# State outputs of both steps of a tile together, the chain's value in PSUM, and the output projection begun beside the last attention block

## The chip, the cores and the metric

One program runs on one core of a Trainium2 chip. The metric is the device time of one execution in microseconds, as the median of several runs. Five engines work side by side and wait for each other on semaphores: TensorE (PE; its weight loads are listed apart as PEld), VectorE (DVE), ScalarE (ACT), GpSimd (POOL), and SyncE (SP), which issues most transfers.

## The reference

The kernel computes a chain of transformer-like blocks over a sequence of 512 positions and a width of 1024: an attention block with compressed and windowed keys ("nsa"), a state-space block ("s5"), and a second network (a stick-breaking and retention mixer, a convolutional feed-forward, a gated linear attention mixer, and again a feed-forward). The change touches the end of the first block and the second. In short form:

```python
h = x + nsa_mixer(rmsnorm(h, l0_norm), ...)        # ends with  mix @ l0_w_out
# s5 mixer, with u, z = split(rmsnorm(h, l1_norm) @ l1_w_in)
#   per 32 channels: complex diagonal state, 
#   state[t] = lambda_bar * state[t-1] + B_bar u[t]
#   y[t] = Re(C state[t]) + D u[t]
#   out = glu(gelu(y) @ l1_w_glu) * silu(z) @ l1_w_out
h = h + s5_mixer(rmsnorm(h, l1_norm), ...)
```

## The kernel before

**Weights.** All weight matrices are cut into tiles of 128 output features by 1024 inputs. SP streams them into a ring of four buffers `raw` (`sp_stream`, `sp_tiles`). For each tile DVE makes the rounded high part (`split_tile`, `whi`, L171), POOL subtracts it from the original to get the low part (`wlo`, L151, L163, L1688, L2496), and TensorE makes 24 multiplications per tile: eight chunks of the inputs by three (high by high, high by low, low by high). `whi` and `wlo` have two buffers each, so the cast of tile t+2 waits until tile t is done (`tile_done`). The accumulators are PSUM banks 0 and 1.

**The attention block.** Eight pairs of heads by four blocks of queries make 32 steps M (`pe_macro`, `act_macro`, `dve_macro`). In each step TensorE turns the probabilities (L1277), and multiplies them by the values (L1289), with quarters of a projection tile put between (`pe_beside`); steps 30 and 31 have no such tile. After the last step ACT takes the gate (`act_nsa_z`, L1428, with two activation tables loaded), DVE multiplies (`dve_mix`, `nmix`), ACT makes the high half (`act_nsa_hi`, `nh`), and POOL the low half (`rest`, `nl`, L1702). POOL's low parts of the first two tiles of the output projection come after that, in its general stream.

**The output projection** ("nsa_out", `pe_residual`, `dve_residual`): eight tiles m, each of 24 multiplications. After each tile DVE casts the tile after next, adds to the residual `h` (L401), adds a square (L237), and does a piece of the preparation for the state-space block, `s5_setup(dve, j)` after tile j. A piece is a complex product of "taps": two multiplies of 128x1024 elements into `wtmp` (`tap_product`, L2168) and two sums of 128x512. Pieces 0 to 3 are the input taps, piece 4 the first output taps; before piece 0 come eight small copies (`tap_coefficient`). The raw taps are fetched by two transfers on ACT's queue (`act_s5_loads`), issued when tile 0 is done. Then the norm begins (L288).

**The state-space block.** Eight input tiles (`input_tile`) give `su`; SP shuffles each with 16 small transfers into `ub`. DVE goes on with taps and tables between the casts. The loop has 16 steps g, two for each tile f = g // 2 of 128 channels. In each step TensorE computes the inputs to the states of the next step (`pe_inputs`, L2533), DVE runs the chain (`s5_chain`, L2401 to L2419): multiply by a rotation `se`, a scan along time (L2408), multiply back, and write the states `sx`. TensorE then adds the outputs of the states (`pe_states`, L2556) into bank 6. That is, per step, 16 multiplications of 128 moving columns, each split into two instructions, for two groups q of 32 output rows in turn. On the side TensorE turns the next tile's taps (`pe_taps_turn`, L2506, even steps), makes its short kernels (`pe_kernels`, L2517 and L2519, odd steps), multiplies them in (`pe_lags`, L2543, odd steps), and does half of a further projection tile (`product_beside`, L595 to L597, 12 multiplications per step). ACT empties the banks, POOL makes the rotations (`pool_s5`, six operations of 128x256 per step) and one `wlo` per tile. After the loop come the gated unit (L2598) and the output.

In each step of the chain DVE waits for the step before; `sx` has one buffer for each parity of g.

Of the kernel before, what the change touches and what calls it, by code (L numbers as in the profile page):

```python
# [9 lines left out]
ALU = mybir.AluOpType  # L10
# [37 lines left out]
def build(nc, A, out, names=tuple(s[0] for s in STAGES)):  # L48
# [5 lines left out]
    with ExitStack() as ctx:  # L54
# [27 lines left out]
        epsc = tables[:, 2 * P:2 * P + 1]  # L82
        base = (nc.sbuf_base + 63) // 64 * 64
# [1138 lines left out]
        def pe_beside(pe, M, half):  # L1222

            if nsa_tile(M) is None:
                return
# [11 lines left out]
            if second == 1 and half == 1:  # L1237
                mm.then_inc(tile_done, 1)

# [108 lines left out]
        def act_nsa(act):  # L1348
# [62 lines left out]
            act_nsa_z(act, PAIRS - 1)  # L1411
# [53 lines left out]
        def act_macro(act, M):  # L1465
# [6 lines left out]
            if m == 2 and i < PAIRS - 1:  # L1472
                act_nsa_q(act, i + 1)
            if m == 3 and i < PAIRS - 1:
                act_cmp_exp(act, i + 1)
# [206 lines left out]
        def pool_nsa(pool):  # L1682
# [24 lines left out]
            for i in range(PAIRS):  # L1707
# [5 lines left out]
                if i < PAIRS - 1:  # L1713
                    low(7 + 2 * i)
            rest(PAIRS - 1)
# [439 lines left out]
        def act_s5_loads(act):  # L2155
            act.wait_ge(tile_done, T0["nsa_out"] + 1)
# [113 lines left out]
        def tap_product(dve, to, frm, re, im, conj):  # L2270

            (to_re, to_im), _ = taps_of(to, conj)
            _, x = taps_of(frm, conj)
            for k, coef in enumerate((re, im)):
                a = twice[:, coef].rearrange("p f c q -> p f (c q)").rearrange("p f (e h) -> p f e h", h=1)
                tt(dve, tap_tmp[k], x, a.broadcast_to([P, KC, 8, 16]), ALU.mult)
            by_re, by_im = tap_tmp
            tt(dve, to_re, by_re[:, :, 0:4, :], by_im[:, :, 4:8, :], ALU.add if conj else ALU.subtract)
            tt(dve, to_im, by_re[:, :, 4:8, :], by_im[:, :, 0:4, :], ALU.subtract if conj else ALU.add)

# [22 lines left out]
        def s5_input_taps(dve, j):  # L2303

            if j == 0:
                for k, v in enumerate((cre, cim, abre, abim)):
                    tap_coefficient(dve, k, v)
                dve.wait_ge(s_bc, 32)
                tap_product(dve, 0, 0, t_cre, t_cim, False)
            else:  # L2310
                tap_product(dve, j, j - 1, t_are, t_aim, False)
# [62 lines left out]
        def s5_setup(dve, j):  # L2374

            if j < 4:
                s5_input_taps(dve, j)
            if j == 4:
                s5_output_taps(dve, 0)
                s5_output_taps(dve, 1)  # L2380
# [3 lines left out]
        TURN, KERN = (4, 5), 7  # L2384
# [6 lines left out]
        def s5_chain(dve, g):  # L2391

            a, b = sp_[:], sb_[:]
            e_r, e_i = (se[:, g % 2, c:c + 1, :].broadcast_to([P, 2, 2 * KB]) for c in range(2))
# [6 lines left out]
            nc.vector.tensor_tensor(a, bu, e_r, ALU.mult)  # L2401
# [621 lines left out]
```

## Time and profile before

| | |
|---|---|
| median of 3 runs | 2085.98 us (2081.94 to 2087.9) |
| profiled execution | 2086.61 us, span of its records 2084.8 us |
| TensorE busy | 1981.5 us, 95% of the span |
| DVE / ACT / POOL busy | 55% / 29% / 39% |
| end of the attention to the norm | 365.9 to 432.0 us |
| state-space loop | 500.9 to 635.2 us |

Times in the rows are us from the start of the span. An engine's busy time counts a weight load apart. The number in brackets is how long the engine sat idle before the instruction, and what ended it. Ends of TensorE's multiplications are modelled, so their starts are what is compared.

### The profile page before, as it was taken

What the parts mean: (1) busy time and instruction counts of PE and PEld (TensorE: products, weight loads), DVE (VectorE), ACT (ScalarE), POOL (GpSimd) and SP (SyncE); (2) the same over time, 40 slices, a digit from 0 to 9 for tenths busy, and PEclk for the clock granted to TensorE, in tenths of its full rate; (3) what the DMA queues carried; (4) which work ended last, traced back from release to release, by engine and by line L of the source; (5) the groups of instructions that cost most, each with busy time, mean ns of one, the idle gap of its engine ahead of it and who ended that gap; (6) DMA issues with size and microseconds to landing.
All of it is one profiled execution on the core that took longest, in us unless ns stands there. A gap on an engine that the chain in (4) does not pass through costs nothing.

```text
span 2084.8 us, 26851 instructions
## 1 busy us (share of the span) xinstructions
PE 1981.5 (95%) x9924; PEld 1549.0 (74%) x9924; DVE 1143.3 (55%) x2063; ACT 608.3 (29%) x1164; POOL 813.7 (39%) x430
## 2 busy tenths in 40 slices
PE   8999999778999997999999999999999999999999
PEld 5867776656777875666768888888578878888887
DVE  5679998676994434555455454512443355454411
ACT  3136655134552114445422111100322222111100
POOL 3532221345773442222224444444233334444444
PEclk9999999998999998999999999999999999999999
DMA  5620100212102222111112232233212222232232
GB/s 185 172 68 32 41 32 21 91 57 62 65 31 71 91 93 84 51 51 61 61 61 93 91 101 93 99 104 109 67 67 81 71 80 93 91 101 92 99 131 71
DMA packets 55300, 167.64 MB, mean 80 GB/s; under 512 B 8080, under 2 KB 16144, under 8 KB 54816
## 3 DMA queue, kind: packets, MB, share of 16 engines
q1 hardware_dynamic: 47904, 155.22, 22.5%
q10 hardware_dynamic: 7296, 11.08, 1.9%
q8 instruction: 65, 1.06, 0.2%
q14 instruction: 35, 0.29, 0.0%
HBM read 157.88 MB, written 2.10 MB: 77 GB/s over the span
## 4 chain that ended last, share of the span: by engine, by line
issue 40%; PE 33%; POOL 15%; DVE 11%; ACT 1%; POOLq 0%; DVEq 0%; ACTq 0%
POOL wlo L163 14%; PE bank L180 7%; PE bank L181 7%; PE bank L182 7%; DVE prob L1640 2%; DVE ssb L1627 1%; PE bank L2598 1%; PE bank L2600 1%; PE bank L2599 1%; DVE wtmp L2168 1%; PE bank L1264 1%; DVE sb__134 L2413 1%; DVE sb__134 L2408 1%; PE bank L1289 1%; DVE sp__133 L2411 1%
## 5 line engine op out<-in xcount | busy, mean ns | idle before, releaser
L163 POOL TENSOR_TENSOR wlo<-raw,whi 128x1024 fp32r<-128x1024 f32 x252 | 607.1, 2409 | 972.6 <-DVE whi L171 972.6
L171 DVE CAST whi<-raw 128x1024 fp32r<-128x1024 f32 x288 | 203.4, 706 | 407.8 <-PE bank L182 237.4
L180 PE MATMUL bank<-xh,whi 128*128 128x512 f32 x704 | 276.5, 393 | 9.4 <-POOL wlo L163 9.4
L181 PE MATMUL bank<-xl,whi 128*128 128x512 f32 x704 | 275.6, 391 | 0.0
L182 PE MATMUL bank<-xh,wlo 128*128 128x512 f32 x704 | 275.3, 391 | 0.0
L595 PE MATMUL bank<-xh,whi 128*128 128x512 f32 x424 | 177.3, 418 | 1.5 <-POOL wlo L163 1.5
L597 PE MATMUL bank<-xh,wlo 128*128 128x512 f32 x424 | 165.9, 391 | 0.0
L596 PE MATMUL bank<-xl,whi 128*128 128x512 f32 x424 | 165.3, 390 | 0.0
L180 PEld LDWEIGHTS bank<-xh,whi 128*128 128x128 f32 x704 | 133.2, 189 | 38.9 <-POOL wlo L163 10.7
L182 PEld LDWEIGHTS bank<-xh,wlo 128*128 128x128 f32 x704 | 133.2, 189 | 28.0
L181 PEld LDWEIGHTS bank<-xl,whi 128*128 128x128 f32 x704 | 133.3, 189 | 27.3
L180 PE MATMUL bank<-ghi,whi 128*128 128x512 f32 x352 | 136.9, 389 | 0.0
L181 PE MATMUL bank<-glo,whi 128*128 128x512 f32 x352 | 136.9, 389 | 0.0
L182 PE MATMUL bank<-ghi,wlo 128*128 128x512 f32 x352 | 136.9, 389 | 0.0
L1688 POOL TENSOR_TENSOR wlo<-raw,whi 128x1024 fp32r<-128x1024 f32 x20 | 47.3, 2365 | 148.1 <-DVE whi L171 148.1
L595 PEld LDWEIGHTS bank<-xh,whi 128*128 128x128 f32 x424 | 79.7, 188 | 28.0 <-issue 13.5
L597 PEld LDWEIGHTS bank<-xh,wlo 128*128 128x128 f32 x424 | 79.6, 188 | 17.8
L596 PEld LDWEIGHTS bank<-xl,whi 128*128 128x128 f32 x424 | 79.9, 188 | 16.2 <-issue 2.2
L1640 DVE TENSOR_SCALAR prob<-prob,gsig,stat 128x128 f32<-128x128 f32 (+3 forms) x128 | 87.3, 724 | 2.3
L477 DVE TENSOR_TENSOR upad<-bank,rstd 128x512 f32<-128x512 f32 x44 | 30.5, 693 | 102.4 <-PE bank L182 87.4
L224 ACT ACTIVATE bank<-h 128x512 f32<-128x512 f32 x42 | 25.2, 602 | 207.0 <-DVE h L401 200.6
L490 DVE TENSOR_TENSOR bank<-bank,rstd 128x512 f32<-128x512 f32 x44 | 30.8, 700 | 99.4 <-PE bank L182 94.2
(387 smaller groups left out, 3995.5 us busy)
## 6 DMA issues: line engine op xcount, KB each, us to landing
raw<-in_weights_dram SPq DMA_DIRECT2D x288, 512.0 KB, 3.3
h<-in_x_dram SPq DMA_DIRECT2D x2, 1024.0 KB, 7.1
sz<-su SPq DMA_DIRECT2D x128, 16.0 KB, 1.8
out_dram<-h ACTq DMA_DIRECT2D x4, 512.0 KB, 2.6
etab<-in_even_tables_dram ACTq DMA_DIRECT2D x1, 1730.0 KB, 6.5
x_kh<-kvc_h ACTq DMA_DIRECT2D x2, 256.0 KB, 5.1
x_kl<-kvc_l ACTq DMA_DIRECT2D x2, 256.0 KB, 7.3
x_vh<-kvc_h ACTq DMA_DIRECT2D x2, 256.0 KB, 5.0
```

What stands on the lines that cost most here:

```text
L163: nc.gpsimd.tensor_tensor(wlo[:, s % 2, :], raw[:, s, :], whi[:, s % 2, :].bitcast(F32), ALU.subtract).then_inc(w_lo, 1)
L171: nc.vector.tensor_copy(whi[:, t_of_4 % 2, :], raw[:, t_of_4, :]).then_inc(w_hi, 1)
L180: nc.tensor.matmul(to, w_h, pe_h, start=first and k == 0, stop=False)
L181: nc.tensor.matmul(to, w_h, pe_l, start=False, stop=False)
L182: last_mm = nc.tensor.matmul(to, w_l, pe_h, start=False, stop=last and k == chunks - 1)
L477: nc.vector.tensor_tensor(upad[:, 2:], acc[0][:], rstd[:], ALU.mult).then_inc(acc_free[0], 1)
L490: nc.vector.tensor_tensor(gv, acc[1][:], rstd[:], ALU.mult).then_inc(acc_free[1], 1)
L595: nc.tensor.matmul(to[:], w_h, xh[:, k, :], start=k == 0, stop=False)
L596: nc.tensor.matmul(to[:], w_h, xl[:, k, :], start=False, stop=False)
L597: mm = nc.tensor.matmul(to[:], w_l, xh[:, k, :], start=False, stop=k == KC - 1)
L1640: mul = nc.vector.tensor_scalar(prob[:, br, hd, 0:w], prob[:, br, hd, 0:w], gsig[:, qb, g:g + 1], stat[:, 8 + 2 * br + hd:9 + 2 * br + hd] ...
L1688: nc.gpsimd.tensor_tensor(wlo[:, r % 2, :], raw[:, r % 4, :], whi[:, r % 2, :].bitcast(F32), ALU.subtract).then_inc(w_lo, 1)
```

## The change

- The first five chunks of tile 0 of the output projection are put into the last attention step (three behind its first turned block, two behind its second). The rest of tile 0 and tile 1 are ordered so that what needs the last pair's low half comes late: chunks 5 and 6 of tile 0, chunks 0 to 2 of tile 1, chunk 7 of tile 0, chunks 3 to 7 of tile 1.
- POOL makes the low parts of those two weight tiles before the last pair's low half. ACT's gate of the last pair moves to step 30. The two transfers of the taps are issued when the last product is done, ahead of ACT's high half.
- The taps' products are cut: after each tile DVE does one multiply and the two sums, or two multiplies, or two sums with one multiply, over all eight tiles; the small copies come before tile 0.
- The chain's value lies in PSUM bank 7 in place of the SBUF buffer `sb_`; the kernels move from bank 7 to bank 4, which they share with half of the turned taps, with waits on both sides.
- State outputs are computed once per tile, for both steps, with the four groups of 32 rows innermost; so are the kernels. `xd` needs 32 columns in place of 128, and one full multiplication adds it.
- The first kernels come after input tile 7, and ACT copies the first turned taps one tile earlier.

```diff
             if nsa_tile(M) is None:
+                if M == LAST:
+                    pe_nsa_out_chunks(pe, 0, ((0, 1, 2), (3, 4))[half])
                 return
...
                 mm.then_inc(tile_done, 1)
+
+        def pe_nsa_out_chunks(pe, m, chunks):
+
+            for k in chunks:
+                if k == 0:
+                    pe.wait_ge(w_lo, T0["nsa_out"] + m + 1)
+                    pe.wait_ge(acc_free[m], (O0["nsa_out"] + m) // 2 + 1)
+                    if m == 0:
+                        pe.wait_ge(acc_free[1], freed(O0["nsa_rest"] + 19))
+                    if m == 1:
+                        pe.wait_ge(n_mix, PAIRS)
+                pe.wait_ge(n_lo, k + 1)
+                mm = pe_out_chunk(pe, m, k, nh, nl)
+            if k == KC - 1:
+                mm.then_inc(tile_done, 1)
+
+        def pe_nsa_out(pe, n):
+
+            pe_nsa_out_chunks(pe, 0, (5, 6))
+            pe_nsa_out_chunks(pe, 1, (0, 1, 2))
+            pe_nsa_out_chunks(pe, 0, (7,))
+            pe_nsa_out_chunks(pe, 1, (3, 4, 5, 6, 7))
+            for m in range(2, KC):
+                pe.wait_ge(w_lo, T0["nsa_out"] + m + 1)
+                pe.wait_ge(acc_free[m % 2], (O0["nsa_out"] + m) // 2 + 1)
+                for k in range(KC):
+                    mm = pe_out_chunk(pe, m, k, nh, nl)
+                mm.then_inc(tile_done, 1)
+            pe_squares(pe, n)
...
                 act_macro(act, M)
-            act_nsa_z(act, PAIRS - 1)
+            act_s5_loads(act)
             act_nsa_hi(act, PAIRS - 1)
...
                 act_nsa_q(act, i + 1)
+            if m == 2 and i == PAIRS - 1:
+                act_nsa_z(act, i)
             if m == 3 and i < PAIRS - 1:
...
                     low(7 + 2 * i)
+            low(20)
+            low(21)
             rest(PAIRS - 1)
...
         def act_s5_loads(act):
-            act.wait_ge(tile_done, T0["nsa_out"] + 1)
+            act.wait_ge(n_mix, PAIRS)
             for slot, what in ((2 * LB - 2, "s5_b"), (8, "s5_c")):
...
-            if j < 4:
-                s5_input_taps(dve, j)
+            if j == 0:
+                dve.wait_ge(s_bc, 32)
+                tap_multiplied(dve, 0, 0, t_cre, False)
+                tap_multiplied(dve, 1, 0, t_cim, False)
+            if j == 1:
+                tap_sums(dve, 0, False)
+                tap_multiplied(dve, 0, 0, t_are, False)
+            if j == 2:
+                tap_multiplied(dve, 1, 0, t_aim, False)
+                tap_sums(dve, 1, False)
+            if j == 3:
+                tap_multiplied(dve, 0, 1, t_are, False)
+                tap_multiplied(dve, 1, 1, t_aim, False)
             if j == 4:
+                tap_sums(dve, 2, False)
+                tap_multiplied(dve, 0, 2, t_are, False)
+            if j == 5:
+                tap_multiplied(dve, 1, 2, t_aim, False)
+                tap_sums(dve, 3, False)
+            if j == 6:
                 s5_output_taps(dve, 0)
-                s5_output_taps(dve, 1)
+                tap_multiplied(dve, 0, 0, t_are, True)
+            if j == 7:
+                tap_multiplied(dve, 1, 0, t_aim, True)
+                tap_sums(dve, 1, True)
 
         STEPS5 = 2 * KC
         GLU = (0, 1, 2, 3)
-        TURN, KERN = (4, 5), 7
+        TURN, KERN, CHAIN = (4, 5), 4, 7
...
             a, b = sp_[:], sb_[:]
+            x = bank[CHAIN].rearrange("p (c t) -> p c t", c=2)
             e_r, e_i = (se[:, g % 2, c:c + 1, :].broadcast_to([P, 2, 2 * KB]) for c in range(2))
...
                 dve.wait_ge(s_xim, g)
-            nc.vector.tensor_tensor(a, bu, e_r, ALU.mult)
+            nc.vector.tensor_tensor(x, bu, e_r, ALU.mult)
             nc.vector.tensor_tensor(b, bu, e_i, ALU.mult).then_inc(s_free, 1)
             dve.wait_ge(s_free, g + 1)
-            nc.vector.tensor_tensor(a[:, 0, :], a[:, 0, :], b[:, 1, :], ALU.add).then_inc(s_r, 1)
-            nc.vector.tensor_tensor(a[:, 1, :], a[:, 1, :], b[:, 0, :], ALU.subtract).then_inc(s_r, 1)
+            nc.vector.tensor_tensor(x[:, 0, :], x[:, 0, :], b[:, 1, :], ALU.add).then_inc(s_r, 1)
+            nc.vector.tensor_tensor(x[:, 1, :], x[:, 1, :], b[:, 0, :], ALU.subtract).then_inc(s_r, 1)
             dve.wait_ge(s_r, 2 * g + 2)
             dve.wait_ge(s_dk, 2 * g + 2)
-            nc.vector.tensor_tensor_scan(b.rearrange("p c t -> p (c t)"), dk[g % 2][:], a.rearrange("p c t -> p (c t)"), 0.0,
-                                         ALU.mult, ALU.add).then_inc(s_v, 1)
+            nc.vector.tensor_tensor_scan(bank[CHAIN], dk[g % 2][:], bank[CHAIN], 0.0, ALU.mult, ALU.add).then_inc(s_v, 1)
             dve.wait_ge(s_v, g + 1)
-            nc.vector.tensor_tensor(a, b, e_r, ALU.mult).then_inc(s_q, 1)
+            nc.vector.tensor_tensor(a, x, e_r, ALU.mult).then_inc(s_q, 1)
             dve.wait_ge(s_q, 2 * g + 1)
-            nc.vector.tensor_tensor(b, b, e_i, ALU.mult).then_inc(s_q, 1)
+            nc.vector.tensor_tensor(x, x, e_i, ALU.mult).then_inc(s_q, 1)
             dve.wait_ge(s_q, 2 * g + 2)
             if g >= 2:
-                dve.wait_ge(s_y, g - 1)
-            pairs = [in_pairs(x) for x in (a, b)]
+                dve.wait_ge(s_y, g // 2)
+            pairs = [in_pairs(v) for v in (a, x)]
             nc.vector.tensor_tensor(sx[:, g % 2, 0, :, 1:], pairs[0][:, 0], pairs[1][:, 1], ALU.subtract)
...
             pe.wait_ge(s_xc, 3 * f + 3)
-            if f:
-                pe.wait_ge(s_kd, 4 * f)
-            for q in range(4):
-                rows = slice(32 * q, 32 * q + 32)
-                for c in range(2):
-                    nc.tensor.matmul(bank[KERN][rows, 0:LB * 32], xb[:, c, q, LB - 1, :], xc[:, f % 2, 0:LB, c, rows],
-                                     start=c == 0, stop=False)
-                mm = nc.tensor.matmul(bank[KERN][rows, 0:32], ident[:, rows], xd[:, rows], start=False, stop=True)
+            pe.wait_ge(s_bt, 2 * f + 1)
+            for c in range(2):
+                for q in range(4):
+                    rows = slice(32 * q, 32 * q + 32)
+                    mm = nc.tensor.matmul(bank[KERN][rows, 0:LB * 32], xb[:, c, q, LB - 1, :], xc[:, f % 2, 0:LB, c, rows],
+                                          start=c == 0, stop=False)
+            mm = nc.tensor.matmul(bank[KERN][:, 0:32], ident, xd[:, 0:32], start=False, stop=True)
             mm.then_inc(s_k, 1)
...
-        def pe_states(pe, g):
-
-            f = g // 2
-            pe.wait_ge(s_xim, g + 1)
+        def pe_states(pe, f):
+
+            pe.wait_ge(s_xim, 2 * f + 2)
             for r in range(LB):
                 for c in range(2):
-                    for o in range(2):
-                        q = 2 * (g % 2) + o
+                    for q in range(4):
                         rows = slice(32 * q, 32 * q + 32)
                         mm = nc.tensor.matmul(bank[6][rows, r * KB:(r + 1) * KB], xc[:, f % 2, r + 1, c, rows],
-                                              sx[:, g % 2, c, o, 0:KB], start=False, stop=r == LB - 1 and c == 1)
+                                              sx[:, q // 2, c, q % 2, 0:KB], start=False, stop=r == LB - 1 and c == 1)
             mm.then_inc(s_y, 1)
...
             pe_taps_turn(pe, 0)
+            input_tile(7)
             pe_kernels(pe, 0)
-            input_tile(7)
             pe_inputs(pe, 0)
             for g in range(STEPS5):
                 f = g // 2
                 if g % 2:
                     pe_lags(pe, f)
-                if g:
-                    pe_states(pe, g - 1)
+                elif g:
+                    pe_states(pe, f - 1)
                 if g + 1 < STEPS5:
...
                 if t == 0:
-                    pe_states(pe, STEPS5 - 1)
+                    pe_states(pe, KC - 1)
             for t in range(2):
...
                     act_nsa(act)
-                    act_residual(act, "nsa_out", n + 1, beside=lambda: act_s5_loads(act))
+                    act_residual(act, "nsa_out", n + 1)
                     continue
...
                     pe_nsa(pe)
-                    pe.wait_ge(acc_free[1], freed(O0["nsa_rest"] + 19))
-                    pe_residual(pe, "nsa_out", after, lambda k: pe.wait_ge(n_lo, k + 1),
-                                rhs=[(lambda k: nh[:, k, :], lambda k: nl[:, k, :])])
+                    pe_nsa_out(pe, after)
                 if name == "s5":
...
+        def tap_multiplied(dve, k, frm, coef, conj):
...
+            tt(dve, tap_tmp[k], x, a.broadcast_to([P, KC, 8, 16]), ALU.mult)
...
+        def tap_sums(dve, to, conj):
...
             tt(dve, to_re, by_re[:, :, 0:4, :], by_im[:, :, 4:8, :], ALU.add if conj else ALU.subtract)
             tt(dve, to_im, by_re[:, :, 4:8, :], by_im[:, :, 0:4, :], ALU.subtract if conj else ALU.add)
...
+                pe.wait_ge(s_kd, 4 * f)
...
-            nc.scalar.activation(xd[:], ident, ACT.Copy, scale=sd[:, f:f + 1]).then_inc(s_xc, 1)
+            nc.scalar.activation(xd[:, 0:32], in_group, ACT.Copy, scale=sd[:, f:f + 1]).then_inc(s_xc, 1)
...
-            act_turned_taps(act, 0)
+                if j == 6:
+                    act_turned_taps(act, 0)
...
-                first = T0["nsa_out"]
+                first = T0["nsa_out"] + 2
...
-    t = np.zeros((P, 2 * P + 8), np.float32)
+    t = np.zeros((P, 2 * P + 40), np.float32)
+    t[:, 2 * P + 8:] = np.arange(P)[:, None] % 32 == np.arange(32)[None, :]
```

## Rows read from the trace of the kernel before

**Rows 1.** Busy time by stretch: us, busy time (instructions) of each engine, clock, DMA.

```profile
421.00:426.00 5.00, 5.00 (x23) 4.12 (x23) 1.50 (x3) 0.60 (x1) 2.41 (x1) 1.00 0.50 161
517.70:620.80 103.10, 96.60 (x865) 79.56 (x864) 100.94 (x121) 55.74 (x110) 79.77 (x78) 1.00 0.15 48
620.80:635.20 14.40, 12.73 (x105) 10.33 (x106) 14.09 (x18) 2.14 (x3) 8.10 (x7) 1.00 0.20 71
```

**Rows 2.** Timeline around the end of the attention: start, us, instruction [idle before <-releaser].

```profile
356.71 0.49 ACT L1463 ACTIVATE probt<-bank 128x384 f32<-128x384 f32 x1 [3.41 <-PE bank L1277]
...
363.89 1.97 PE L1289 MATMUL bank<-probt,nin 128*64 128x128 f32 x32
...
364.61 1.28 ACT L1428 ACT_TABLE_LOAD   x1
...
366.59 0.69 DVE L1658 TENSOR_TENSOR nmix<-bank,nin 128x512 f32<-128x512 f32 x1 [2.34 <-ACT nin L1428]
...
367.82 0.63 ACT L1434 ACTIVATE nh<-nmix 128x512 fp32r<-128x512 f32 x1
...
368.52 1.26 POOL L1702 TENSOR_TENSOR nl<-nmix,nh 128x512 fp32r<-128x512 f32 x1 [20.65 <-ACT nh L1434]
...
369.74 4.66 POOL L163 TENSOR_TENSOR wlo<-raw,whi 128x1024 fp32r<-128x1024 f32 x2
...
372.18 0.76 PE L180 MATMUL bank<-nh,whi 128*128 128x512 f32 x1 [6.33 <-issue]
```

**Rows 3.** Timeline of the output projection, ACT's queue and DVE.

```profile
380.17 0.69 ACTq L2158 DMA_DIRECT2D taps<-in_s_c_dram  x1
...
385.90 2.48 DVE L2168 TENSOR_TENSOR wtmp<-taps,twice 128x1024 f32<-128x1024 f32 x2 [1.67 <-DMA taps<-in_s_c_dram]
...
396.58 0.69 DVE L171 CAST whi<-raw 128x1024 fp32r<-128x1024 f32 x1
...
403.46 0.69 DVE L171 CAST whi<-raw 128x1024 fp32r<-128x1024 f32 x1
...
426.58 0.69 DVE L171 CAST whi<-raw 128x1024 fp32r<-128x1024 f32 x1 [4.08 <-PE bank L182]
...
431.97 0.76 DVE L288 SCALAR_TENSOR_TENSOR bank<-h,gains,bank 128x512 f32<-128x512 f32 x1 [3.49 <-ACT bank L256]
```

**Rows 4.** Timeline at the start of the state-space loop, DVE and TensorE.

```profile
500.18 0.69 DVE L171 CAST whi<-raw 128x1024 fp32r<-128x1024 f32 x1 [8.69 <-DMA raw<-in_weights_dram]
...
500.93 2.97 PE L2533 MATMUL bank<-sz,bt 128*128 128x128 f32 x16 [2.33 <-ACT bt L2648]
```

**Rows 5.** Timeline of one odd step of the loop, TensorE.

```profile
526.43 1.94 PE L2556 MATMUL bank<-sx,xc 128*32 128x128 f32 x32
...
528.30 1.16 PE L2533 MATMUL bank<-sz,bt 128*128 128x128 f32 x8
...
529.39 0.66 PE L2517 MATMUL bank<-xc,xb 128*32 128x128 f32 x6
...
530.75 0.50 PE L595 MATMUL bank<-xh,whi 128*128 128x512 f32 x1
...
534.88 0.52 PE L2556 MATMUL bank<-sx,xc 128*32 128x128 f32 x6 [1.10 <-DVE sx L2419]
```

**Rows 6.** Timeline of DVE in the loop.

```profile
502.22 0.69 DVE L2401 TENSOR_TENSOR sp__133<-bank,se 128x512 f32<-128x512 f32 x1 [1.35 <-PE bank L2533]
...
504.34 1.23 DVE L2408 TENSOR_TENSOR_SCAN sb__134<-ssq,sp__133 128x512 f32<-128x512 f32 x1
...
506.32 0.69 DVE L2413 TENSOR_TENSOR sb__134<-sb__134,se 128x512 f32<-128x512 f32 x1
...
507.94 0.69 DVE L2401 TENSOR_TENSOR sp__133<-bank,se 128x512 f32<-128x512 f32 x1
...
531.24 2.79 DVE L2413 TENSOR_TENSOR sb__134<-sb__134,se 128x512 f32<-128x512 f32 x1
```

**Rows 7.** Groups of instructions: count, busy us and mean ns, idle before.

```profile
L2556 PEld LDWEIGHTS bank<-sx,xc 128*32 128x32 f32 x512 | 26.8, 109 | 12.5 <-DVE sx L2419 10.9 <-issue 0.7
```

More of the change, by code:

```diff
@@ L82, in build @@
         epsc = tables[:, 2 * P:2 * P + 1]
+        in_group = tables[:, 2 * P + 8:2 * P + 40]
         base = (nc.sbuf_base + 63) // 64 * 64
@@ L2268, in tap_coefficient @@
                 ts(dve, twice[:, j, :, c, :], v.rearrange("p (f q) -> p f q", q=4), 1.0, 0.0, ALU.mult, ALU.add)
-        def tap_product(dve, to, frm, re, im, conj):
+        def tap_multiplied(dve, k, frm, coef, conj):
+            _, x = taps_of(frm, conj)
+            a = twice[:, coef].rearrange("p f c q -> p f (c q)").rearrange("p f (e h) -> p f e h", h=1)
+            tt(dve, tap_tmp[k], x, a.broadcast_to([P, KC, 8, 16]), ALU.mult)
+        def tap_sums(dve, to, conj):
             (to_re, to_im), _ = taps_of(to, conj)
[L2273 to L2276, printed above, removed]
             by_re, by_im = tap_tmp
@@ L2279, in tap_product @@
             tt(dve, to_im, by_re[:, :, 4:8, :], by_im[:, :, 0:4, :], ALU.subtract if conj else ALU.add)
+        def tap_product(dve, to, frm, re, im, conj):
+            tap_multiplied(dve, 0, frm, re, conj)
+            tap_multiplied(dve, 1, frm, im, conj)
+            tap_sums(dve, to, conj)
         def s5_coefficients(dve):
@@ L2301, in s5_input_coefficients, with s5_tap_coefficients @@
             tt(dve, mag4, mag2, mag2, ALU.mult)
[L2303 to L2311, printed above, removed]
+        def s5_tap_coefficients(dve):
+            for k, v in enumerate((cre, cim, abre, abim)):
+                tap_coefficient(dve, k, v)
         def s5_output_taps(dve, j):
@@ L2632, in act_taps_out @@
             if f >= 2:
-                act.wait_ge(s_y, 2 * f - 2)
+                act.wait_ge(s_y, f - 1)
             for half in range(2):
@@ L2670, in act_gelu @@
         def act_gelu(act, f):
-            act.wait_ge(s_y, 2 * f + 2)
+            act.wait_ge(s_y, f + 1)
             if f >= 2:
@@ L2855, in _ @@
                     dve_nsa(dve)
+                    s5_tap_coefficients(dve)
                     dve_residual(dve, "nsa_out", ORDER[N_S5],
```

## The prediction

> **What bounds the kernel now.** I read the busy time of each engine by stretch first, then the timelines of the two stretches that the change touches, whose brackets say what each idle time waited for. TensorE is busy nearly everywhere, so a change is worth what TensorE stops waiting for, plus what TensorE itself no longer does. One full-array multiplication of 512 columns costs 0.22 to 0.23 us (23 in 5.00 [rows 1]), and a weight tile of 24 costs 5.46.
>
> Two places hold gaps. TensorE ends the last attention block at 365.86 (363.89 + 1.97) and starts tile 0 of the output projection only at 372.18 [rows 2]: ACT's gate, DVE's product, ACT's high half and POOL's low half come first, and then POOL's two weight subtractions (4.66) queued behind them. After that DVE sets the pace: its casts come every 6.88 us (396.58, 403.46 [rows 3]) against 5.46 of TensorE. In the state-space loop a tile takes 17.2 us (six in 103.10), of which TensorE works 16.1 (96.60/6) and DVE 16.8 (100.94/6) [rows 1]. DVE is the bound there, and TensorE waits 1.10 for sx in each tile [rows 5].
>
> **The change in the output projection.** (a) Five of tile 0's eight chunks, 15 multiplications = 3.4 us, go into the last block. I credit nothing for idles that they may fill and put the end of the attention at 369.2. (b) The two weight subtractions move to a time when POOL is idle. The second, 2.33, stands beside DVE's scaling of prob, whose operands all lie in SBUF. Such an operation stands still while POOL works: a multiply of 512 elements took 2.79 beside a subtraction and 0.69 alone [rows 6]. The slip is between 0 and 2.3. ACT, which waits for the same turned block as DVE, idles 3.41 just then, so there is slack, and I count nothing on top of (a). (c) ACT's gate with its two table loads takes 3.2 (364.61 to 367.82). It moves into those 3.41, so it costs nothing, and DVE's 2.34 of waiting for it goes; without that cover it costs up to 3.2. (d) Two DMA issues of 0.69 now stand on ACT's queue ahead of the last high half. From 369.25: product 0.69, issues 1.38, high half 0.63, low half 1.26 = 373.3. TensorE meanwhile has 15 multiplications (chunks 5 and 6, and three of tile 1), waits 0.7, ends tile 0 at 374.0 and tile 1 at 377.4. The taps, issued by 371, land 5.0 later, as before (380.86 to 385.90 [rows 3]): 376.
>
> (e) The eight small coefficient copies go ahead of tile 0, where DVE waits for it, and cost nothing. The taps' products are spread over eight tiles. A 128x1024 multiply costs 1.24 (two in 2.48), so a tile with one fewer takes DVE 6.88 - 1.24 = 5.64. That is 0.2 over TensorE's 5.46, but with two weight buffers a cast may be 2.3 late (5.46 less cast 0.69 and subtraction 2.4) before TensorE stops. The cast after tile 1 comes at 379.7 (cast 374.1, residual add, POOL's subtraction until 377.2, then two multiplies): 2.3 late, just covered. Five casts at 5.6 and one at 4.6 follow (tile 6 has one multiply and a short sign change): the last cast at 412.3, TensorE at 410.7. Before, the norm began 5.39 after that cast, and DVE waited 3.49 of it for the exponential [rows 3]. The last third (a multiply and two sums of 0.7) now sits in that wait, behind POOL's subtraction (3.1 from the cast): 5.8. So the norm begins at 418.1 instead of 431.97: **13.9**. Bounds: 9 with the whole slip of (b) and later landings, 17 if DVE has no backlog.
>
> **The change in the state-space stage.** Up to its input tile 6 the same instructions follow the norm and shift with it; from here I write the times of before. (f) Head: TensorE waited 2.33 for ACT's bt before the first inputs at 500.93. Now bt is copied during input tile 7, and the inputs start near 497.7. The gain is not 3.2, because the first chain also needs DVE past a cast that waits for weights until 500.18 [rows 4], behind SP's queue of block transfers, which is unchanged. Chain 0 starts at 500.9, 1.3 earlier, two chains end at 512.1, and the loop's first states start there instead of with the second step's at 517.7: **5.6**.
>
> (g) Chain value in PSUM. Free of POOL, a chain took 5.7 from start to start (502.22 to 507.94, scan 1.23 [rows 6]). With one operand in PSUM an operation took 0.69 as with none, so the multiplies keep 0.69 and lose the 2.79. No row shows a scan in PSUM: 1.23 is the lower bound, and for the upper I let it grow by a third, to 1.6. I take 1.23 and a chain of 5.6. Two chains, a cast and yl (0.7 each) make 12.6 per tile.
>
> (h) States of both steps together. Now 32 instructions take 1.87 (526.43 to 528.30), 58 ns each, in two column groups in turn; full-array ones of the same width take 136 ns (8 in 1.09 [rows 5]). Four in turn are in no row. The bounds are 64 at 29 ns = 1.87 for both steps, and 64 at 58 = 3.7. The nearest row, two in turn, halves the price without loss, so I take 29 ns: 1.87 less per tile. The kernels (1.36, 529.39 to 530.75) are put in turn too: 18 instructions, 0.75, 0.6 less (bound: 0.2 less). TensorE then needs 16.1 - 1.87 - 0.6 = 13.6, above DVE's 12.6, and becomes the bound. What is late next: states(f) wait for both chains. Counted from the start of states(f-1): inputs end at 3.0, chain 2f at 6.3, yl at 7.0, chain 2f+1 at 12.6, one us before it is wanted. ACT empties the shared bank of turned taps and kernels in the same order as before, with TensorE's products between. POOL, 13.3 per tile now (79.77/6), stands behind DVE less. Six tiles at 17.2 - 13.6 = 3.6: **21.5**.
>
> (i) Tail: 14.4 from the states to the gated unit [rows 1]; now 10.9, without step 14's states and the wait before them: **3.5**. The last 64 instructions take the time of the 32 that stood there.
>
> Sum: 13.9 + 5.6 + 21.5 + 3.5 = 44.5. The profiled execution took 2086.6 (span 2084.8) and the median is 2086.0: 2042.1 against the first, **2041.5** against the second. Later stages are untouched.
>
> A page of the Trainium skill speaks against (h): "TensorE: Matmul & The Clock Gate", Part 3, says that a weight load overlaps running multiplications only where the row group differs, and here every load has all rows. By that rule the loads would lie bare. The trace disagrees for two column groups: a load lasts 109 ns [rows 7] and one is done every 58. The same page measured 2.38 times for three column tiles, 0.79 of three; an estimate by it is 2.35 for (h) in place of 1.87, 4 us less in all.
>
> **Rivals.** (A) Four column groups are no faster than two. For: 29 ns would mean 4.4 columns per ns, while the densest streams of the trace, two in turn (128/0.058) and the 512-column ones (512/0.22), both stay at 2.2 to 2.3. Against: the halving was clean. TensorE needs 15.7 per tile: 1.5 x 6 = 9, head 5.6, tail 1.6, less 1.9 at the last states, plus 13.9 = 28: 2058. (B) DVE stays the bound: PSUM makes the scan 1.6 and the other eight operations 0.08 slower, chain 6.6, 14.6 per tile: 6 less, 2048. It decides from a chain of 6.1. Against: 0.69 with and without PSUM. (C) The projection gives half, DVE's backlog and the delayed attention eating 7: 2049. (D) Slower: with four groups in turn nothing overlaps, so a load of 0.11 and a multiply of 0.11 stand one after another. The states are 64 instructions in eight tiles, 512 in all; at 29 ns the gain is 44.5, and each 0.01 us more takes 5.1 back. It decides from 0.116 us; at 0.22 it is 53 slower: 2139. Against: 58 ns with two groups. (E) No change: the wait for both chains or a fallen clock swallows it all; nothing in the rows for it.
>
> **Numbers.** Forecast 0.60 (own range 2034 to 2049), A 0.16, B 0.11, C 0.07, D 0.03, E 0.03. A measurement of this kernel cannot tell 0.3% (6 us) from no change. Only D and E are not faster by more: faster 0.94, same 0.03, slower 0.03. The range reaches A and the forecast's better end (17 in the projection, 13.2 per tile): 2032 to 2060.
>
> **What would show it.** In the changed profile: tile 0's multiplications inside the last block and no gap of 6 us after it; casts 5.5 to 5.7 apart; the norm near 418; 64 state instructions in 1.9; a loop period near 13.6 without waits for sx; scans at 1.23 and no multiply of 2.8. Wrong would be a period above 15 (A if TensorE is full, B if DVE is), casts at 6.8, or a norm after 423.

## The result and the profile after

The changed kernel takes **2057.8 us** (median of 4 runs, 2056.7 to 2062.3) against 2086.9 for the kernel before beside it (2081.9 to 2088.7): ratio 0.987, 95% interval 0.986 to 0.989. The forecast was 2041.5, so 29 of the 44.5 us came. The profiled execution took 2057.75 (span 2055.9), 28.9 less than the profiled one of before. That difference is what the stages below have to add up to.

The output projection, timeline of DVE, answers [rows 3] (start, us, instruction, idle before and its releaser):

```profile
373.54 0.70 DVE L172 CAST whi<-raw 128x1024 fp32r<-128x1024 f32 x1 [2.87 <-PE bank L991]
...
378.97 0.69 DVE L172 CAST whi<-raw 128x1024 fp32r<-128x1024 f32 x1
...
411.55 0.68 DVE L172 CAST whi<-raw 128x1024 fp32r<-128x1024 f32 x1
...
418.72 0.76 DVE L289 SCALAR_TENSOR_TENSOR bank<-h,gains,bank 128x512 f32<-128x512 f32 x1 [1.52 <-ACT bank L257]
```

The casts come every 5.4 to 5.6 us instead of 6.88, and the norm begins at 418.72 instead of 431.97: 13.25 us.

The head of the loop, timelines of DVE and TensorE, answers [rows 4]:

```profile
488.34 0.69 DVE L172 CAST whi<-raw 128x1024 fp32r<-128x1024 f32 x1 [10.13 <-DMA raw<-in_weights_dram]
...
500.32 2.56 PE L2613 MATMUL bank<-sx,xc 128*32 128x128 f32 x64 [2.10 <-DVE sx L2478]
```

The first chain again stands behind a cast that waits for weights, and that cast moved by 11.8 us (500.18 to 488.34) where the norm moved by 13.25. The first states start at 500.32.

The loop, timeline of TensorE, answers [rows 5]:

```profile
515.36 1.96 PE L2613 MATMUL bank<-sx,xc 128*32 128x128 f32 x64
...
525.02 0.64 PE L2576 MATMUL bank<-xc,xb 128*32 128x128 f32 x16
...
525.84 0.48 PE L596 MATMUL bank<-xh,whi 128*128 128x512 f32 x1
...
528.78 1.96 PE L2613 MATMUL bank<-sx,xc 128*32 128x128 f32 x64
...
545.76 3.57 PE L2613 MATMUL bank<-sx,xc 128*32 128x128 f32 x64 [3.49 <-DVE sx L2478]
```

64 state instructions now take 1.89 us up to the next inputs (515.36 to 517.25), as 32 did before, and the short kernels take 0.82 instead of 1.36. An undisturbed tile takes 13.42 us (515.36 to 528.78). But the next one takes 16.98, and the states that end it wait 3.49 for DVE. DVE's own timeline says why:

```profile
527.36 0.41 DVE L2478 TENSOR_TENSOR sx<-sp__133,bank 128x256 f32<-128x256 f32 x1
533.40 0.69 DVE L172 CAST whi<-raw 128x1024 fp32r<-128x1024 f32 x1 [5.63 <-DMA raw<-in_weights_dram]
...
536.13 1.23 DVE L2468 TENSOR_TENSOR_SCAN bank<-ssq,bank 128x512 f32<-128x512 f32 x1
```

The scan in PSUM takes 1.23, as in SBUF [rows 6]. The cast waits 5.63 us for a weight slab, and two chains stand behind it. The queue of SP at that time:

```profile
496.77 10.00 SPq L146 DMA_DIRECT2D sz<-su  x16
506.82 0.58 SPq L128 DMA_DIRECT2D raw<-in_weights_dram  x1
507.50 22.16 SPq L146 DMA_DIRECT2D sz<-su  x32
530.02 2.07 SPq L136 DMA_DIRECT2D raw<-in_weights_dram  x4
```

SP issues its transfers one after another, some 0.65 us each (16 in 10.00, 32 in 22.16). Four slabs stand between the block transfers, and the next behind all of them, issued at 530.02 and landed 3.4 later. That slab is wanted when DVE ends its chain, at 527.8. In the kernel before it was not late: issued at 541.28, and wanted by a cast that began at 551.93 without a wait.

The busy time by stretch shows that the wait has a second price (us, busy us and instructions of PE, PEld, DVE, ACT, POOL, then TensorE's granted clock):

```profile
528.78:545.76 16.98, 13.49 (x139) 10.81 (x138) 12.02 (x21) 10.66 (x21) 9.14 (x13) 1.00 0.36 128
545.76:549.40 3.64, 3.64 (x65) 3.26 (x66) 3.57 (x6) 0.02 (x1) 3.64 (x6) 0.53 0.46 149
549.40:560.82 11.42, 11.42 (x75) 8.99 (x75) 8.91 (x15) 7.52 (x15) 9.05 (x12) 1.00 0.07 19
560.82:574.24 13.42, 13.42 (x140) 10.81 (x139) 12.37 (x20) 9.04 (x18) 9.05 (x12) 1.00 0.07 25
```

After TensorE's idle 3.49 us its granted clock is 0.53, near the 1.2 GHz level, for the next 3.64 us, and the states take 3.57 instead of 1.96. With 3.56 in the one tile and 1.64 in the next (15.06 instead of 13.42), the slab costs 5.2 us. The loop's first tile has the same mark: its states had waited 2.10, the granted clock over their first 3.64 us was 0.67, and the tile took 15.04, 1.6 more than an undisturbed one.

The tail from the last tile of the loop to the gated unit takes 10.5 instead of 14.3 (3.8 for the forecast's 3.5). At the start of the gated unit the changed kernel is 37.0 us ahead (598.18 against 635.16). At the end it is 28.9 ahead. So 8.1 us go in stages of which the prediction said "Later stages are untouched". Busy time from the gated unit to TensorE's last products, kernel after:

```profile
598.18:2051.60 1453.42, 1411.96 (x6188) 1106.15 (x6187) 631.50 (x969) 339.77 (x553) 551.44 (x231) 0.99 0.25 84
```

and kernel before:

```profile
635.16:2080.50 1445.34, 1403.38 (x6156) 1104.54 (x6155) 630.42 (x967) 340.19 (x553) 551.13 (x231) 0.99 0.25 84
```

TensorE is 8.6 us busier with the same work, at the same granted clock. (The 32 more instructions are the last states, which stand in this stretch for both steps now and take no longer.) The groups of instructions tell where (count, busy us, mean ns of one; 1400 to 1435 us, a down projection). Kernel before:

```profile
L182 PE MATMUL bank<-ghi,wlo 128*128 128x512 f32 x52 | 20.2, 389 | 0.0
```

Kernel after:

```profile
L183 PE MATMUL bank<-ghi,wlo 128*128 128x512 f32 x50 | 19.8, 395 | 0.0
```

The span of one product overlaps the next. From start to start it is 226.7 ns before and 233.3 after, worked out from the starts of 132 products (29.92 and 30.80 us). So it is with the products of `ghi`, `glo`, `eo_h`, `eo_l`, `ohi`, `olo`, `nh` and `nl`, and not with those of `xh` and `xl`, which keep 227 in both. The first group starts at the beginning of a stage's own buffers. The change makes the `tables` 32 columns wider, which moves all these buffers by 128 bytes a partition; `xh`, `xl` and the weights lie ahead of the tables and did not move.

### The profile page after: what moved, and what is told of

The parts are those of the page before. It is cut to its first block, busy times and chain, and to the rows that moved or that the text cites. A ratio compares the mean times of both kernels' runs of the same rounds, so it can differ in the third digit from the quotient of the medians.

```text
span 2055.9 us, 26747 instructions
## 1 busy us (share of the span) xinstructions
PE 1969.3 (96%) x9876; PEld 1531.0 (74%) x9876; DVE 1113.0 (54%) x2063; ACT 607.0 (30%) x1164; POOL 793.9 (39%) x430
## 4 chain that ended last, share of the span: by engine, by line
issue 38%; PE 34%; POOL 15%; DVE 8%; SPq 4%; DMA 0%; POOLq 0%; ACT 0%; DVEq 0%; ACTq 0%
POOL wlo L164 14%; PE bank L181 7%; PE bank L182 7%; PE bank L183 7%; SPq L146 4%; DVE prob L1674 2%; DVE ssb L1661 2%; PE bank L2655 1%; PE bank L2656 1%; PE bank L2657 1%; PE bank L1296 1%; PE bank L1321 1%; PE bank L1239 1%; PE bank L1237 1%; DVE probt L1682 1%
```

## The experiments

Two suspects are on the table: the place of the buffers, and SP's queue. The first four kernels ran side by side on one chip, but not beside the change itself. So differences to the change are given from the medians, and by the ratios, each to the kernel before beside it.

**e1_addresses_back**: the 128 bytes are taken from a scratch tile, so that the stages' buffers lie where they did before.

```diff
-        seedt = sb("seedt", [P, 64])
+        seedt = sb("seedt", [P, 32])
```

(and the eight columns of it in use from 40 up moved to 8 up, column 47 of another use to 16)

> The changed kernel with one small scratch tile made 128 bytes a partition smaller, so that every stage's buffers start again where they start in the kernel before (the change had moved them by 128 bytes, by making the tables 32 columns wider); instructions and their order unchanged. Theory 'place': the 232 to 234 ns between the products of ghi, glo, eo_h, ohi, nh in the changed kernel, against 226 to 228 before, come from where these operands lie. Then the pace goes back to 227, and 192 products each in three output projections and 528 in each of the two down projections give 1632 x 6.5 ns = 10.6 us, less what other waits hide: 2047 to 2050 us. Rival 'chip': the slower pace is that of the clock or of this execution: no change, 2056 to 2060 us.

Measured: 2051.3 us, ratio 0.9839 (0.9823 to 0.9854) where the change has 0.9874 (0.9859 to 0.9888): 6.5 less than the change by the medians, 7 by the ratios. The group is back at its mean:

```profile
L183 PE MATMUL bank<-ghi,wlo 128*128 128x512 f32 x52 | 20.2, 389 | 0.0
```

and from the gated unit on the kernel takes what the kernel before took, 1445.5 us:

```profile
600.21:2045.70 1445.49, 1402.99 (x6189) 1105.34 (x6187) 631.16 (x968) 339.72 (x553) 550.70 (x231) 0.99 0.25 84
```

The gain stays under the expected 8 to 11, since the loop lost 2 us more here: the same cast waited 7.04 for its slab instead of 5.63.

**e4_before_moved**: the same from the other side, in the kernel before.

```diff
-        base = (nc.sbuf_base + 63) // 64 * 64
+        base = (nc.sbuf_base + 63) // 64 * 64 + 128
```

> The kernel before, with every stage's buffers 128 bytes a partition further on and nothing else changed. Theory 'place': its projections go at 233 ns a product instead of 227, 10.6 us more by the same count: 2094 to 2098 us. Rival 'chip': 2084 to 2088 us.

Measured: 2094.7 us, ratio 1.0046 (1.0034 to 1.0059), 10.6 slower. One constant, no instruction changed. Single executions scatter by some us: the profiled one was the fastest of its six (2091.1) and shows 4.5 us, not 10, more from the gated unit on than the profiled one of before, though its products of `ghi` and `glo` do start 233 ns apart. With the medians, e1_addresses_back and places_alone below, the place of the operands is shown as the cause.

**e2_tile12_early**: one slab goes ahead of the last block.

```diff
-                    if 2 <= j < 2 + RING:
+                    if 2 <= j < 3 + RING:
```

(the three slabs behind it are written out after the blocks, and the loop of loads starts a group later)

> The changed kernel, with the load of the thirteenth slab from the stage's start issued by SP before the last of the eight block transfers instead of behind it. Theory 'queue': the 5.63 us that DVE waits at 533.4 for that slab is SP's serial issue of 128 block transfers; the loop's tiles of 16.98 and 15.06 us fall to 13.4, so 4 to 5.5 us: 2052 to 2054 us. Rival: the wait moves on to the next slab, which still stands behind all blocks, or the tile is bound by the block transfers themselves: less than 1.5 us.

Measured: 2052.5 us, ratio 0.9841 (0.9826 to 0.9857), 5.3 less by the medians, 7 by the ratios. The queue of SP, and the cast on DVE that had waited 5.63:

```profile
507.62 10.87 SPq L150 DMA_DIRECT2D sz<-su  x16
518.53 1.21 SPq L129 DMA_DIRECT2D raw<-in_weights_dram  x1
519.84 10.01 SPq L150 DMA_DIRECT2D sz<-su  x16
529.89 2.43 SPq L132 DMA_DIRECT2D raw<-in_weights_dram  x3
```

```profile
528.54 0.95 DVE L176 CAST whi<-raw 128x1024 fp32r<-128x1024 f32 x1 [0.63 <-PE bank L602]
```

The order of one transfer was the wait, and it did not move on to the next slab: all tiles behind the first take 13.42, and the gated unit starts at 592.64 instead of 598.18. The first tile still takes 15.06, with the granted clock at 0.54 over its first 3.65 us.

**e3_both**: both edits, and the slabs among the blocks one block earlier each (`if 1 <= j < 3 + RING`, slab `first + j - 1`).

> Both edits together, and the slabs loaded between the blocks each one block earlier (so that the 10.13 us wait of the cast at 488.3 shrinks too). Theories 'place' and 'queue' together: 10 + 5 + 1 to 3 us: 2039 to 2043 us. If either fails, its part is missing: 2047 or 2051.

Measured: 2037.3 us, ratio 0.9765 (0.975 to 0.978), 2 us better than expected; again in a later set of runs, **both_again**, 2037.0, ratio 0.978 (0.977 to 0.979).

> The kernel of the third experiment once more, to stand beside the next two on the same chip: 2035 to 2039 us.

Six tiles of the loop, from the first states on:

```profile
497.82:578.18 80.36, 80.36 (x829) 64.89 (x828) 73.51 (x120) 54.13 (x107) 62.84 (x78) 1.00 0.20 63
```

13.39 us a tile, TensorE without a gap and at full clock, DVE 12.25 a tile. This is the loop that the prediction described (13.6 and 12.6), in a kernel that takes 47 us less than the one before. The slabs one block earlier are worth some 4 us of that, on top of the two repairs of e1 and e2: the first states start at 497.82 instead of 500.32, and the first tile takes 13.4 instead of 15.04.

With the disturbances gone, the parts of the change can be priced one by one, each taken out of e3_both. The prices do not add up, since taking one part out changes which engine is the bound.

**two_in_turn**: the states in the order of the steps, so that two column groups take turns.

```diff
-            for r in range(LB):
-                for c in range(2):
-                    for q in range(4):
+            for step in range(2):
+                for r in range(LB):
+                    for c in range(2):
+                        for q in range(2 * step, 2 * step + 2):
```

> The third experiment's kernel (places and queue mended) with the 64 state instructions of a tile ordered by steps, so that two row groups take turns and not four. Theory of the prediction (TensorE is the bound of the loop, four in turn halve the price): 64 go from 1.9 to 3.7 us in each of eight tiles, so the period goes from 13.4 to 15.2 and the time up by 13 to 15 us: 2050 to 2052. Rival: the four in turn are issued but another wait (DVE's chain of 12.6 per tile) hides most of it: less than 6 us more.

Measured: 2050.9 us, 13.6 more than e3_both. The tile takes 14.75 (515.42 to 530.16), and its states:

```profile
515.42 3.30 PE L2618 MATMUL bank<-sx,xc 128*32 128x128 f32 x64
```

Up to the next inputs they take 3.22 (1.89 with four in turn), 50 ns each and not 58. The starts of the single instructions say why: in both kernels each column group starts one every 110 ns, about one load (109 ns [rows 7]), and the second pair of groups begins 1.37 us after the first, whose last starts come at 1.70; in between, four groups run here too. So four in turn are worth 1.35 us a tile and not 1.87, 10.8 us over eight tiles. The rest of the 13.6 is not the states': in this execution an instruction ahead of the edit (the last scores of the attention) already came 2.7 us later than in e3_both.

**chain_in_sbuf**: `s5_chain` works in `sp_` and `sb_` again.

```diff
-            nc.vector.tensor_tensor(x, bu, e_r, ALU.mult)
+            nc.vector.tensor_tensor(a, bu, e_r, ALU.mult)
...
-            nc.vector.tensor_tensor_scan(bank[CHAIN], dk[g % 2][:], bank[CHAIN], 0.0, ALU.mult, ALU.add).then_inc(s_v, 1)
+            nc.vector.tensor_tensor_scan(b.rearrange("p c t -> p (c t)"), dk[g % 2][:], a.rearrange("p c t -> p (c t)"), 0.0, ALU.mult, ALU.add).then_inc(s_v, 1)
```

(and so for the sums and the multiplies back)

> The third experiment's kernel with the chain value of the state recurrence back in SBUF, as in the kernel before; the PSUM bank stays idle. Theory of the prediction: the multiply that stands behind POOL's subtraction costs again 2.8 instead of 0.7 us once in a step or so, DVE needs 12.6 + 2 x 1.3 to 2.1 = 15 to 17 us a tile against TensorE's 13.4, and the time goes up by 10 to 25 us: 2047 to 2062. Rival: TensorE's 13.4 us covers it, since POOL subtracts one slab a tile only: less than 3 us more.

Measured: 2067.6 us, ratio 0.992 (0.991 to 0.993), 30.3 more than e3_both and 5 above the expected range. The second chain of a tile on DVE, POOL beside it, and five tiles by busy time:

```profile
528.77 0.83 DVE L2468 TENSOR_TENSOR sp__133<-sp__133,sb__134 128x256 f32<-128x256 f32 x1
529.64 1.63 DVE L2471 TENSOR_TENSOR_SCAN sb__134<-lnv,sp__133 128x512 f32<-128x512 f32 x1
531.31 1.05 DVE L2473 TENSOR_TENSOR sp__133<-sb__134,se 128x512 f32<-128x512 f32 x1
532.39 2.76 DVE L2475 TENSOR_TENSOR sb__134<-sb__134,se 128x512 f32<-128x512 f32 x1
```

```profile
530.16 1.65 POOL L2555 TENSOR_TENSOR se<-se,setmp 128x256 f32<-128x256 f32 x1
531.77 2.82 POOL L2558 TENSOR_TENSOR wlo<-raw,whi 128x1024 fp32r<-128x1024 f32 x1
```

```profile
518.84:604.64 85.80, 75.36 (x691) 61.20 (x691) 84.08 (x101) 43.72 (x88) 67.27 (x65) 0.90 0.13 42
```

Not only the one multiply stands behind POOL (2.76 instead of 0.69 [rows 6]): the sums (0.83 instead of 0.42) and the scan (1.63 instead of 1.23) are stretched too. DVE is busy 98% and sets 17.16 us a tile, TensorE waits, and its granted clock falls to 0.90. With the chain in SBUF a tile takes as long as before the whole change (17.2), so the gain per tile hangs on the PSUM bank; four groups in turn and the cheaper kernels pay only once DVE is under TensorE.

**taps_whole**: `s5_setup` with a whole product beside each of the first four tiles, and two output steps beside the fifth.

```diff
+            if j == 0:
+                dve.wait_ge(s_bc, 32)
+                tap_product(dve, 0, 0, t_cre, t_cim, False)
+            elif j < 4:
+                tap_product(dve, j, j - 1, t_are, t_aim, False)
```

> The third experiment's kernel with the tap products placed whole beside the blocks of the output projection, as in the kernel before, and not in thirds. Theory: DVE's slots beside blocks 0 to 3 go from 5.5 to 6.9 us and that beside block 4 to about 8.5, while blocks 5 to 7 stay with TensorE's 5.4; the norm begins 2.5 to 4 us later and the time goes up by that: 2039.5 to 2041.5. Rival: the whole projection slows down as before the change (13 us), which would say that the gain was in the taps alone: 2050.

Measured: 2042.4 us, 5.1 more. DVE's casts:

```profile
374.25 0.69 DVE L176 CAST whi<-raw 128x1024 fp32r<-128x1024 f32 x1 [2.87 <-PE bank L995]
381.12 0.69 DVE L176 CAST whi<-raw 128x1024 fp32r<-128x1024 f32 x1
387.97 0.69 DVE L176 CAST whi<-raw 128x1024 fp32r<-128x1024 f32 x1
...
425.01 0.75 DVE L293 SCALAR_TENSOR_TENSOR bank<-h,gains,bank 128x512 f32<-128x512 f32 x1 [5.19 <-ACT bank L261]
```

6.86 a cast again, and the norm 50.8 us after the first cast instead of 45.1. I had expected 2.5 to 4: the four slots of 6.86 cost 5.3 us over those of e3_both, and the three casts behind them, 16.3 us where e3_both has 15.9, gave none of it back.

**no_early_chunks**: none of the projection's products beside the last attention block.

```diff
-                if M == LAST:
-                    pe_nsa_out_chunks(pe, 0, ((0, 1, 2), (3, 4))[half])
...
-            pe_nsa_out_chunks(pe, 0, (5, 6))
+            pe_nsa_out_chunks(pe, 0, (0, 1, 2, 3, 4, 5, 6))
```

> The third experiment's kernel without the products of the output projection that stand beside the last attention block: the 15 of its first five chunks are done after that block with the others. Theory: after the block TensorE does 15 products and then waits 0.5 us for nl; 15 more take 3.4 us, of which 0.5 lay in that wait, and the norm behind the projection begins 2.9 us later: 2040 us. Rival: TensorE's slots beside the block were free but DVE's casts and taps set the cadence of the projection, so that less than 1 us is lost: 2037.5.

Measured: 2041.3 us, ratio 0.979 (0.977 to 0.980) against 0.978 (0.977 to 0.979) for both_again beside it. The medians are 4 apart, about what was expected, but the intervals overlap; the traces decide on the projection. In no_early_chunks TensorE's last attention products and DVE's first cast:

```profile
363.70 1.97 PE L1323 MATMUL bank<-probt,nin 128*64 128x128 f32 x32
...
373.41 0.69 DVE L176 CAST whi<-raw 128x1024 fp32r<-128x1024 f32 x1 [5.40 <-PE bank L995]
```

In e3_both:

```profile
366.27 1.97 PE L1325 MATMUL bank<-probt,nin 128*64 128x128 f32 x32
...
373.45 0.69 DVE L176 CAST whi<-raw 128x1024 fp32r<-128x1024 f32 x1 [2.87 <-PE bank L995]
```

The early products put off the end of the attention by 2.57 us. What they save behind it, they cost ahead of it: the first cast is at 373.4 in both, and the norm at 418.5 and 418.6. Counted from the last scores of the attention, which come before the edit, the first cast is 18.6 us and the norm 63.7 or 63.8 us later in all three traces (both_again too). The 4 us between the medians show in the traces behind the gated unit, where the kernels are the same: 1448.4 us to the end against 1443.6 in both_again, and 1448.5 in e3_both.

**places_alone**: what the place costs, by itself. Groups of instructions of TensorE alone, 96 products in each line, from one execution; in the order of the lines shown, the 512-column operand and the weights start at 0 and 64, 0 and 128, 192 and 128, 128 and 128, and 0 and 0 bytes past a multiple of 256.

> Nothing of the reference is computed: TensorE alone does 24 runs of 96 products of 512 columns (three per chunk as in the kernel, each with its weight load), which differ only in where the 512-column operand starts (131072 bytes + 128, 0, 32, 64, 96, 160, 192, 224, 256, 320, 384, 448, 640, 1152) and where the weights start (81920 bytes + 128; then 0, 32, 64, 192, 256, 384 with the operand at 128; 0, 64, 256 with it at 0). Theory 'place': the pace takes 227 or 233 ns (or other steps) by the start modulo 256 or 512 bytes, with no other engine running. Rival: it takes other engines' traffic to show it, and all 24 runs go at one pace.

```profile
L105 PE MATMUL bank<-moving,weight 128*128 128x512 f32 x96 | 22.6, 395 | 0.0
...
L85 PE MATMUL bank<-moving,weight 128*128 128x512 f32 x96 | 22.6, 395 | 0.0
...
L90 PE MATMUL bank<-moving,weight 128*128 128x512 f32 x96 | 22.1, 391 | 0.0
...
L107 PE MATMUL bank<-moving,weight 128*128 128x512 f32 x96 | 21.9, 389 | 0.0
L104 PE MATMUL bank<-moving,weight 128*128 128x512 f32 x96 | 21.9, 389 | 0.0
```

From start to start over each run, they come out in three kinds. **226.7 to 227.2 ns** where operand and weights start at the same place modulo 256 bytes (128 and 128, 384 and 128, 640 and 128, 1152 and 128, 128 and 384, 0 and 0, 0 and 256). **229.0** where the operand starts 64 bytes further (192 and 128, 448 and 128, 128 and 64). **232.4 to 234.2** at all other distances tried (32, 96, 128, 160, 192, 224). In these runs it is the distance that counts: an operand at 0 is fast with weights at 0 and slow with weights at 128. (The first of the 24 runs begins slowly, with 11 products in its first 4.7 us, and is not counted.) No other engine ran. Why the distance matters, no run shows.

**glu_places**: the finding applied to `yl`, `gh` and `gl`, which lay 64 bytes off.

```diff
+        used[0] += (base - used[0]) % 256
         taps_base = used[0]
...
-        used[0] = tables_base
+        used[0] = tables_base - 256
```

> The third experiment's kernel, with the operands of the gated unit and of the stage's output projection (yl, gh, gl) moved so that they too start at the weights' place modulo 256 bytes (they started 64 bytes off; yh and yl take turns, so their 384 products went at 232 ns, and the 192 of gh and gl at 229). By what TensorE alone did (226.7 at equal places, 229 at 64 more, 233 at other distances): 384 x 5 + 192 x 2.3 ns = 2.4 us less. Rival: the pace there has another cause (the buffers in rows of 4608 bytes, DVE's and ACT's traffic): the products stay at 229 to 232 and the time within 0.5 us.

The pace came down to 227 ns. Groups from 655 to 680 us, both_again and then glu_places:

```profile
L2660 PE MATMUL bank<-yl,whi 128*128 128x512 f32 x37 | 14.6, 394 | 0.0
```

```profile
L2661 PE MATMUL bank<-yl,whi 128*128 128x512 f32 x38 | 14.8, 389 | 0.0
```

From start to start, the products of `yh` and `yl` went from 232 to 227 ns, and those of `gh` and `gl` from 229 to 227. The 229 is that of places_alone. The 232 it does not explain: `yh` lay at the weights' place and only `yl` 64 bytes off, but the products took turns and all were slow; no run tried operands in turn by themselves.

The total did not follow: 2038.3 us, ratio 0.9775 (0.976 to 0.979) against 0.9779. In its profile the granted clock was 0.89 over the first 30 us of the gated unit, against 1.00 over that whole stage in both_again, and that took more than the 2 us. Whether it falls so in other runs, the one profile doesn't tell; a gain of 0.1% stays unresolved.

## Why the prediction was wrong, point by point

**The queue (steps f, h).** The step that failed is "behind SP's queue of block transfers, which is unchanged". I used that queue for the first cast and then, asking in (h) what is late next, went through DVE, ACT and POOL and left SP out. The queue keeps its own time, 128 transfers of 0.65 us that began 12 us earlier than before, while its reader came to that slab some 23 us earlier (the third tile's states start at 528.78 instead of 552.07). It cost 5.2 us by the trace and 5.3 by e2_tile12_early (7 by the ratios). The head shows the same limit: I let the first chain's cast shift with the norm, but its slab came only 11.8 us earlier and not 13.25. The first states came 17.4 earlier, of which 13.25 is the norm's, so (f) gave 4.1 and not 5.6; and behind their wait of 2.10 the lower clock cost the first tile another 1.6. Both losses are gone in e3_both. A fallen clock behind a wait is what rival E named and found nothing for in the rows.

**The later stages.** "Later stages are untouched" failed: 8.1 us by the trace, 6.5 by e1_addresses_back, 10.6 by e4_before_moved. The instructions were untouched, their operands' addresses were not. The line of the diff that did it (`2 * P + 40`) was on my table, priced at nothing. That is the step that failed here: a term put at nothing without a reason, which measures 8.1 us.

**The output projection (a to e): right in sum, wrong in one reason.** 13.25 against 13.9. The cadence of 5.4 to 5.6 and the norm's time (418.1 forecast, 418.72 measured) came as worked out, the spreading of the taps by itself giving 5.1 by the medians and 5.6 by the trace (taps_whole). One term was too small: from the last cast to the norm it takes 7.17 and not 5.8, which earlier casts (411.55 for 412.3) half made up. And step (a), products into the last block, gives nothing (no_early_chunks); the rest of the gain comes from the moved gate and weight subtractions (b, c), which no run took out one by one.

**States, kernels, chain (g, h): right.** 29.5 ns an instruction for 29, kernels 0.82 for 0.75, scan 1.23, chain 5.6, 13.42 us a tile (13.39 in e3_both) for 13.6. TensorE became the bound. Rival A (four groups no faster than two) falls by the 29.5 ns in the trace and by two_in_turn, 13.6 us slower. Rival B (DVE stays the bound, by a slower scan in PSUM) falls by the scan at 1.23 and DVE's 12.25 in tiles of 13.39; DVE as the bound is what chain_in_sbuf shows once the PSUM bank is taken away, 30 us slower. Rival C falls by the projection's 13.25. The six tiles still gave 15.8 us and not 21.5 (87.3 instead of 103.1), by the waits and the low clock above. The rule of "TensorE: Matmul & The Clock Gate", Part 3, of the Trainium skill, weighed against (h), is not borne out: 64 loads of 109 ns each pass in 1.89 us, under running products that differ in the column group alone.

**The sum.** By the trace 15.6 of the 44.5 us are missing: 0.65 in the projection, 1.5 in the head, 5.7 in the loop, 8.1 in the later stages, less 0.3 gained in the tail. The kernel of e3_both gains 47 us (2084.1 to 2037.3), where 44.5 was forecast; about 4 of these come from the slabs moved a block earlier, which the change does not have. So the parts were right in size, and the two omissions, the queue and the addresses, are nearly all of the miss. The total by itself would have misled: 2057.8 lies in the range of 2032 to 2060, but above the forecast's own 2034 to 2049, in the upper part that was kept for rivals, and it is rival A's 2058 by chance, while the trace refutes A. That the measured time lies in the range is luck.

## What to carry to other kernels

When a loop is made faster, put every queue that feeds it on the list of what is late next, with its own start and its own cadence, SP's too, since a queue that was just in time before is the new bound. Before a diff's declarations are priced at nothing, see what they move: here 128 bytes cost over a quarter of what the change brought (8.1 of 28.9 us). A total that agrees with a rival's number proves nothing before the trace is read. And a wait of TensorE can cost nearly half as much again in the lower clock behind it (3.49 us of waiting, 1.6 us of slower states).

## What was not expected of the hardware

- A product of 512 fp32r columns with its weight load takes 226.7 ns when operand and weights start at the same place modulo 256 bytes, 229.0 with the operand 64 bytes further, and about 233 at the other distances tried, with TensorE alone at work (places_alone, one execution). A shift of one of them against the other by 128 bytes cost this kernel 0.5%.
- Two column groups in turn took 58 ns an instruction over 32 (1.87 us), four took 29.5 over 64 (1.89 us). Each group by itself starts one instruction every 110 ns in both, so the gain comes from the number of groups at work.
- A scan and sums in SBUF are stretched by POOL's work like a multiply (1.63 for 1.23, 0.83 for 0.42); with their value in PSUM none of them is (all 16 scans of e3_both took 1.23).
